# Down projection of a top-2 expert layer: half of its rows on split weights, a second loading queue, and block ends without GpSimd's drain

## The chip, the cores and the metric

One NeuronCore of a Trainium2 chip runs the whole decoder layer as one program. The metric is the device time of an execution in microseconds (us), lower is better. The five engines are PE (TensorE), DVE (VectorE), ACT (ScalarE), POOL (GpSimd) and SP (SyncE, which here only issues DMAs).

## What is computed

A decoder layer on 1024 tokens of 1024 features: a mixer (stick-breaking attention beside gated linear attention), then a mixture of experts, then a last RMSNorm. Only the expert layer matters for the change:

```python
# every token has 2 of 32 experts; the tokens of an expert are padded to whole blocks
def expert_block(args):
    e, x_blk = args
    hidden = jax.nn.silu(x_blk @ exp_w_gate[e]) * (x_blk @ exp_w_up[e])
    return hidden @ exp_w_down[e]          # (block, 512) @ (512, 1024)

yb = lax.map(expert_block, (block_expert, xb))
y = yb.reshape(n_slots, D) * slot_gate[:, None]
out = zeros.at[slot_tok].add(y)
```

Everything is float32. `exp_w_gate` and `exp_w_up` are 1024x512 for an expert, `exp_w_down` 512x1024, 2 MB each.

## The kernel before

The program is a row of blocks (`nc.Block()`), each with one instruction list per engine; at a block's end all engines meet, and POOL first runs an instruction DRAIN. The last three blocks are in `mix_and_route` (output projection, routing), `experts` and `combine` (sum of the two experts' rows, last norm).

`experts` goes over blocks of at most 96 tokens (CAP), 32 of them for these inputs, one an expert. The loop body holds two blocks and runs 15 times; the last two blocks stand behind it. For block b:

- POOL gathers the 96 rows of tokens (`x_g`), PE transposes them (`turn_x`), ACT copies them from PSUM rounded to the single-pass type fp32r (`x_hi`), and DVE subtracts to get the rest (`x_lo`).
- The gate and up weights are split in the same way, in halves of 128x2048: ACT writes `g_hi`/`u_hi`, DVE writes `g_lo`/`u_lo` = raw - hi. PE then makes each product as three fp32r matmuls (hi\*hi, lo\*hi, hi\*lo): 24 matmuls of 128x512 for the gate, 24 for up (`rows`, L1566).
- ACT takes the sigmoid of the gate product, DVE multiplies twice (`gate_mul`, then `up_mul`, which writes `hid`, L1515), PE transposes `hid` (`turn_h`, L1558), ACT copies it to `hidT` (L1451).
- The down projection (`down`, L1590) is plain float32: 4 row groups (KF) x 2 halves of the columns, 8 matmuls, which the compiler makes 16 instructions. ACT moves the result out with the gate factor (`evict`, L1461) and POOL scatters the rows to `y2_dram`.

The order on each engine is written by hand. PE has, for a block: 15 gate matmuls of the next block, `turn_h`, 9 gate matmuls, `down`, 12 up matmuls, `turn_x`, 12 up matmuls:

```python
gate_rows(b + 1, 1 - j, 0, 15)
turn_h(b)
gate_rows(b + 1, 1 - j, 15, 24)
down(b, j, 16 * i + 16)
up_rows(b + 1, 1 - j, 0)
turn_x(j, 16 * i + 32)
up_rows(b + 1, 1 - j, 1)
```

SP loads each half of `w_g` and `w_u` when DVE has made its lower part (semaphores `glo`, `ulo`), and the 2 MB of `w_d` (two buffers) when the down projection before is done (`d_used`).

Of the kernel before, what the change touches and what calls it, by code (L numbers as in the profile page):

```python
# [14 lines left out]
F32 = mybir.dt.float32  # L15
# [922 lines left out]
def mix_and_route(k, c, out_c, cat, tiles, retire):  # L938
# [77 lines left out]

    with nc.Block() as block:
        @block.sync
# [293 lines left out]
def experts(k, c, tables, tiles):  # L1312
# [6 lines left out]
    (w_g, wg, g_in), (w_u, wu, u_in) = weights["g"], weights["u"]  # L1319
    w_d, wd, d_in = sb("w_d", [P, 2, KF, D], F32, c), k["a"]["exp_w_down"][0], [sem(f"e_d_in{m}") for m in range(2)]  # L1320
# [26 lines left out]
    with nc.Block() as block:  # L1347
        @block.sync
        def _(sp):
            def down(j, e):  # L1350
                sp.dma_start(w_d[:, j], wd[bass.ds(e, 1)].rearrange("o (p k) n -> p (o k) n", p=P)).then_inc(d_in[j], 16)
# [6 lines left out]
            down(0, 0)  # L1358
            for m in range(2):
                sp.wait_ge(ulo, m + 1)  # L1360
                load(sp, w_u, wu, 1, m, u_in)
            n_less = sp.value_load(halves[0:1, 1:2], min_val=EXPERTS // 2 - 1, max_val=MAX_HALVES - 1)
            with sp.Fori(0, n_less) as i:
                for j in range(2):
                    b = 2 * i + j
                    e2 = sp.value_load(block_e[0:1, bass.ds(b + 2, 1)], min_val=0, max_val=EXPERTS - 1)
                    e1 = sp.value_load(block_e[0:1, bass.ds(b + 1, 1)], min_val=0, max_val=EXPERTS - 1)
                    for m in range(2):
                        sp.wait_ge(glo, 2 * b + m + 3)
# [62 lines left out]
        def _(act):  # L1432
# [24 lines left out]
            def evict(b, j, i):  # L1457
                act.wait_ge(d_used, b + 2)
# [24 lines left out]
            b = 2 * n_less  # L1483
            u_split(b + 1, 1)
            hid_copy(b)
            sigmoid(b + 1)
            evict(b, 0, n_less)
            hid_copy(b + 1)
            evict(b + 1, 1, n_less)

        @block.vector
        def _(dve):
# [31 lines left out]
            g_split(1, 1)  # L1524
            x_split(1, 1)
            u_split(1, 0)
            n_less = dve.value_load(halves[0:1, 1:2], min_val=EXPERTS // 2 - 1, max_val=MAX_HALVES - 1)
            with dve.Fori(0, n_less) as i:
                for j in range(2):
                    b = 2 * i + j  # L1530
                    up_mul(b)
                    u_split(b + 1, 1)
                    g_split(b + 2, 0)
                    gate_mul(b + 1)
                    g_split(b + 2, 1)
                    x_split(b + 2, j)
                    u_split(b + 2, 0)
            b = 2 * n_less
            up_mul(b)
            u_split(b + 1, 1)  # L1540
            gate_mul(b + 1)
            up_mul(b + 1)

        @block.tensor
        def _(pe):
# [37 lines left out]
            def down(b, j, loaded):  # L1583
                pe.wait_ge(hidT_done, b + 1)
# [9 lines left out]
            pe.sem_inc(d_used, 1)  # L1594
            turn_x(0, 16)
# [32 lines left out]
def combine(k, c, cat):  # L1628
# [77 lines left out]
```

## Time and profile before

| | us |
|---|---|
| median of 3 executions | 1517.08 (1517.06 to 1518.2) |
| the profiled execution | 1505.85 |
| its span, first to last instruction | 1504.1 |
| PE busy in the span | 1271.8 (85%) |
| DVE / ACT / POOL busy | 778.8 / 624.4 / 205.6 |
| mean granted TensorE clock | 0.937 of full speed |

The profiled execution has 1.75 us around its span. The median of the executions without a profile lies 11.2 us above it. `experts` runs from 812 to 1462 us of the span, `combine` behind it. Times within the span are counted from its start. A row of a timeline gives start and length of an instruction; since instructions overlap in an engine's pipeline, the distance of two starts in a dense row ("the pitch") tells the engine's rate better than the length.

### The profile page before, as it was taken

What the parts mean: (1) busy time and instruction counts of PE and PEld (TensorE: products, weight loads), DVE (VectorE), ACT (ScalarE), POOL (GpSimd) and SP (SyncE); (2) the same over time, 40 slices, a digit from 0 to 9 for tenths busy, and PEclk for the clock granted to TensorE, in tenths of its full rate; (3) what the DMA queues carried; (4) which work ended last, traced back from release to release, by engine and by line L of the source; (5) the groups of instructions that cost most, each with busy time, mean ns of one, the idle gap of its engine ahead of it and who ended that gap; (6) DMA issues with size and microseconds to landing.
All of it is one profiled execution on the core that took longest, in us unless ns stands there. A gap on an engine that the chain in (4) does not pass through costs nothing. (4 is left out here: it accounts for less than half of the span.)

```text
span 1504.1 us, 16744 instructions
## 1 busy us (share of the span) xinstructions
PE 1271.8 (85%) x5980; PEld 921.7 (61%) x5980; DVE 778.8 (52%) x786; ACT 624.4 (42%) x695; POOL 205.6 (14%) x222
## 2 busy tenths in 40 slices
PE   4999998868977995769963999999999999999940
PEld 3867676646766685548852666666666666666620
DVE  5163646462357318454466655555555555555407
ACT  6254545444221422231121555555555455555403
POOL 0000000002023004100024022121222221122100
PEclk9999999998998998979975999999999999999975
DMA  5110000002100100072104999999999999999618
GB/s 168 43 29 19 25 1 1 1 3 69 42 14 1 42 14 0 0 294 103 56 29 150 400 368 351 356 342 353 346 340 355 347 338 345 347 357 345 238 42 323
DMA packets 71612, 263.06 MB, mean 175 GB/s; under 512 B 13826, under 2 KB 39444, under 8 KB 51092
## 3 DMA queue, kind: packets, MB, share of 16 engines
q1 hardware_dynamic: 61780, 245.59, 44.4%
q0 software_dynamic: 9792, 16.93, 3.6%
q8 instruction: 26, 0.43, 0.1%
q14 instruction: 14, 0.11, 0.0%
HBM read 249.33 MB, written 21.55 MB: 180 GB/s over the span
## 5 line engine op out<-in xcount | busy, mean ns | idle before, releaser
L1590 PE MATMUL ps<-w_d,hidT 128*96 128x512 f32 x512 | 225.0, 592 | 0.8 <-ACT hidT L1451 0.8
L1496 DVE TENSOR_TENSOR g_lo<-w_g,g_hi 128x2048 fp32r<-128x2048 f32 x62 | 141.7, 2286 | 42.9 <-ACT g_hi L1437 42.9
L1501 DVE TENSOR_TENSOR u_lo<-w_u,u_hi 128x2048 fp32r<-128x2048 f32 x64 | 146.2, 2285 | 27.8 <-ACT u_hi L1443 27.8
L1590 PEld LDWEIGHTS ps<-w_d,hidT 128*96 128x96 f32 x512 | 83.3, 163 | 123.6 <-issue 120.1
L406 DVE TENSOR_TENSOR_SCAN prod<-stay 128x256 f32<-128x256 f32 (+7 forms) x64 | 83.4, 1345 | 86.2 <-ACT beta L358 86.2
L1505 DVE TENSOR_TENSOR x_lo<-ps,x_hi 128x768 fp32r<-128x768 f32 x32 | 30.6, 957 | 187.8 <-ACT x_hi L1447 187.8
L1443 ACT ACTIVATE u_hi<-w_u 128x2048 fp32r<-128x2048 f32 x62 | 118.7, 1914 | 10.6 <-PE ps L1566 7.3
L1437 ACT ACTIVATE g_hi<-w_g 128x2048 fp32r<-128x2048 f32 x62 | 118.1, 1904 | 6.0 <-PE ps L1566 5.9
L1566 PE MATMUL ps<-u_hi,x_hi 128*128 128x512 f32 x256 | 116.3, 454 | 0.0
L1566 PE MATMUL ps<-g_hi,x_hi 128*128 128x512 f32 x256 | 104.8, 409 | 2.0 <-DVE x_lo L1505 2.0
L1566 PE MATMUL ps<-g_lo,x_hi 128*128 128x512 f32 x256 | 101.9, 398 | 0.0
L1566 PE MATMUL ps<-g_hi,x_lo 128*128 128x512 f32 x256 | 101.7, 397 | 0.0
L1566 PE MATMUL ps<-u_lo,x_hi 128*128 128x512 f32 x256 | 101.4, 396 | 0.0
L1566 PE MATMUL ps<-u_hi,x_lo 128*128 128x512 f32 x256 | 101.2, 395 | 0.0
L1461 ACT ACTIVATE y<-ps,where 96x1024 f32<-96x1024 f32 x32 | 35.6, 1112 | 147.6 <-PE ps L1590 147.6
L250 PE MATMUL ps<-h_hi,gw_hi 128*128 128x512 f32 x208 | 83.4, 401 | 12.2 <-DVE gw_lo L710 7.7
L933 POOL DMA_INDIRECT x_g<-h_dram,who x32 | 56.4, 1762 | 216.8 <-DMA where<-slots 198.2
L444 PE MATMUL ps<-h_hi,w_hi 128*128 128x512 f32 x192 | 79.0, 412 | 4.6 <-DVE w_lo L396 4.6
L250 PE MATMUL ps<-h_lo,gw_hi 128*128 128x512 f32 x208 | 82.4, 396 | 0.0
L250 PE MATMUL ps<-h_hi,gw_lo 128*128 128x512 f32 x208 | 82.4, 396 | 0.0
L444 PE MATMUL ps<-h_hi,w_lo 128*128 128x512 f32 x192 | 75.9, 395 | 0.0
L444 PE MATMUL ps<-h_lo,w_hi 128*128 128x512 f32 x192 | 75.6, 394 | 0.0
(272 smaller groups left out, 2285.9 us busy)
## 6 DMA issues: line engine op xcount, KB each, us to landing
w_g<-exp_w_gate SPq DMA_DIRECT2D x64, 1024.0 KB, 6.9
w_u<-exp_w_up SPq DMA_DIRECT2D x64, 1024.0 KB
w_d<-exp_w_down SPq DMA_DIRECT2D x32, 2048.0 KB, 11.4
gw_raw<-w_in SPq DMA_DIRECT2D x13, 512.0 KB
w_raw<-w_in SPq DMA_DIRECT2D x12, 512.0 KB, 3.9
xt<-x SPq DMA_DIRECT2D x8, 512.0 KB, 6.6
x_g<-x SPq DMA_DIRECT2D x8, 512.0 KB, 3.4
h_dram<-h SPq DMA_DIRECT2D x8, 512.0 KB, 2.6
```

The lines of the kernel that those rows point to most:

```text
L250: mm = pe.matmul(out, w[:, kd, :], h[:, kd, cols], start=(n == 0), stop=(n == 3 * KD - 1))
L406: dve.tensor_tensor_scan(prod[:, h, T - nk:T][:, ::-1], x, x, 1.0, ALU.mult, ALU.bypass)\
L444: mm = pe.matmul(out, w[:, t % 2, x // 3, :], h[:, x // 3, cols], start=(x == 0), stop=(x == 3 * KD - 1))
L933: pool.indirect_dma_start(x_g[0:CAP, j, :], None, k["h2_dram"][:, :], bass.IndirectOffsetOnAxis(ap=who[j][0:CAP, 0:1], axis=0), bounds_che ...
L1437: act.activation(g_hi[:, 4 * m:4 * m + 4], w_g[:, 4 * m:4 * m + 4], ACT.Copy).then_inc(ghi, 1)
L1443: act.activation(u_hi[:, 4 * m:4 * m + 4], w_u[:, 4 * m:4 * m + 4], ACT.Copy).then_inc(uhi, 1)
L1461: act.activation(y[j][0:CAP, :], ps[0:CAP, 2:4, :].rearrange("p b n -> p (b n)"), ACT.Copy, scale=where[j][:].bitcast(F32)[0:CAP, 2:3]).th ...
L1496: dve.tensor_tensor(g_lo[:, part], w_g[:, part], g_hi[:, part].bitcast(F32), ALU.subtract).then_inc(glo, 1)
L1501: dve.tensor_tensor(u_lo[:, part], w_u[:, part], u_hi[:, part].bitcast(F32), ALU.subtract).then_inc(ulo, 1)
L1505: dve.tensor_tensor(columns(x_lo[j]), turned_x(), columns(x_hi[j]).bitcast(F32), ALU.subtract).then_inc(xlo_done, 1)
L1566: mm = pe.matmul(out, x_[:, n // 3, :], w_[:, n // 3, :], start=(n == 0), stop=(n == 3 * KD - 1))
L1590: mm = pe.matmul(ps[0:CAP, 2 + m, :], hidT[:, f, :], w_d[:, j, f, cols], start=(f == 0), stop=(f == KF - 1))
```

## The change

1. Row groups 0 and 1 of the down projection are made on split operands. `w_s` (one buffer, 128x2048) takes their weights; ACT makes `s_hi` from it and DVE `s_lo`; the transposed hidden rows of these groups are split as well, into `hT_hi` (ACT) and `hT_lo` (DVE), with 96 columns each. Each of these products is three fp32r matmuls. Row groups 2 and 3 stay plain, with `w_d` now half as large (two buffers of 128x2048) and `hidT` too.
2. ACT asks for the plain half of the weights, in its own queue behind `evict`, and loads the expert's number for it from `block_e`; SP asks for `w_s`, between the two halves of `w_g`.
3. The last three blocks of the program are opened with `no_gpsimd_drain=True`.

```diff
-    with nc.Block() as block:
+    with nc.Block(no_gpsimd_drain=True) as block:      (mix_and_route, experts, combine)
...
                     for m in range(2):
                         sp.wait_ge(glo, 2 * b + m + 3)
                         load(sp, w_g, wg, e2, m, g_in)
-                    sp.wait_ge(d_used, b + 1)
-                    down(1 - j, e1)
+                        if m == 0:
+                            sp.wait_ge(slo, b + 1)
+                            sp.dma_start(w_s[:], wd[bass.ds(e1, 1)].rearrange("o (p k) n -> p (o k) n", p=P)[:, 0:HF])\
+                              .then_inc(s_in, 16)
...
             def hid_copy(b):
                 act.wait_ge(hturned, b + 1)
-                act.activation(hidT[:], turned_h(), ACT.Copy).then_inc(hidT_done, 1)
+                act.activation(hT_hi[:], turned_h()[:, 0:HF], ACT.Copy).then_inc(hidT_done, 1)
+                act.activation(hidT[:], turned_h()[:, HF:KF], ACT.Copy).then_inc(hidT_done, 1)
+
+            def s_split(b, first=False):
+                act.wait_ge(s_in, 16 * b + 16)
+                if not first:
+                    act.wait_ge(d_used, b)
+                act.activation(s_hi[:], w_s[:], ACT.Copy).then_inc(shi, 1)
...
                     evict(b, j, i)
+                    e2 = act.value_load(block_e[0:1, bass.ds(b + 2, 1)], min_val=0, max_val=EXPERTS - 1)
+                    act.dma_start(w_d[:, j], wd[bass.ds(e2, 1)].rearrange("o (p k) n -> p (o k) n", p=P)
+                                  [:, HF:KF]).then_inc(d_in[j], 16)
                     x_split(b + 2, j)
+                    s_split(b + 1)
                     u_split(b + 2, 0)
...
+            def h_split(b):
+                dve.wait_ge(hidT_done, 2 * b + 2)
+                dve.tensor_tensor(hT_lo[:], turned_h()[:, 0:HF], hT_hi[:].bitcast(F32), ALU.subtract).then_inc(hTlo_done, 1)
+
+            def s_split(b):
+                dve.wait_ge(shi, b + 1)
+                dve.tensor_tensor(s_lo[:], w_s[:], s_hi[:].bitcast(F32), ALU.subtract).then_inc(slo, 1)
...
                     up_mul(b)
                     u_split(b + 1, 1)
+                    h_split(b)
                     g_split(b + 2, 0)
                     gate_mul(b + 1)
                     g_split(b + 2, 1)
                     x_split(b + 2, j)
+                    s_split(b + 1)
                     u_split(b + 2, 0)
...
-                for m in range(D // HALF):
-                    cols = slice(m * HALF, (m + 1) * HALF)
-                    for f in range(KF):
-                        mm = pe.matmul(ps[0:CAP, 2 + m, :], hidT[:, f, :], w_d[:, j, f, cols], start=(f == 0),
-                                       stop=(f == KF - 1))
+                for f in range(HF):
+                    for m in range(D // HALF):
+                        cols = slice(m * HALF, (m + 1) * HALF)
+                        pe.matmul(ps[0:CAP, 2 + m, :], hidT[:, f, :], w_d[:, j, f, cols], start=(f == 0), stop=False)
+                pe.wait_ge(hTlo_done, b + 1)
+                pe.wait_ge(slo, b + 1)
+                for f in range(HF):
+                    for n, (x_, w_) in enumerate(((hT_hi, s_hi), (hT_hi, s_lo), (hT_lo, s_hi))):
+                        for m in range(D // HALF):
+                            cols = slice(m * HALF, (m + 1) * HALF)
+                            mm = pe.matmul(ps[0:CAP, 2 + m, :], x_[:, f, :], w_[:, f, cols], start=False,
+                                           stop=(f == HF - 1 and n == 2))
```

Three places of the order that results, the loop body in each case.

DVE before, from the first product with the sigmoid (`gate_mul`) to the product that writes `hid` for `turn_h` (`up_mul`, the last row but one):

```order
L1510 TENSOR_TENSOR hid<-ps,hid 96x512
L1494 REGISTER_ALU
L1496 TENSOR_TENSOR g_lo<-w_g,g_hi 128x2048
L1504 REGISTER_ALU
L1505 TENSOR_TENSOR x_lo<-ps,x_hi 128x8x96
L1501 TENSOR_TENSOR u_lo<-w_u,u_hi 128x2048
L1515 TENSOR_TENSOR hid<-ps,hid 96x512
L1501 TENSOR_TENSOR u_lo<-w_u,u_hi 128x2048
```

The same place of DVE with the change:

```order
L1532 TENSOR_TENSOR hid<-ps,hid 96x512
L1516 REGISTER_ALU
L1518 TENSOR_TENSOR g_lo<-w_g,g_hi 128x2048
L1526 REGISTER_ALU
L1527 TENSOR_TENSOR x_lo<-ps,x_hi 128x8x96
L1545 TENSOR_TENSOR s_lo<-w_s,s_hi 128x2048
L1523 TENSOR_TENSOR u_lo<-w_u,u_hi 128x2048
L1537 TENSOR_TENSOR hid<-ps,hid 96x512
L1523 TENSOR_TENSOR u_lo<-w_u,u_hi 128x2048
L1541 TENSOR_TENSOR hT_lo<-ps,hT_hi 128x192
```

`s_lo` has come between `x_lo` and the `u_lo` that stands ahead of `up_mul`, and `hT_lo` behind it.

ACT before, from the sigmoid to the copy of the turned hidden rows:

```order
L1455 ACTIVATE hid<-ps 96x512
L1437 ACTIVATE g_hi<-w_g 128x2048
L1459 ISA
L1461 ACTIVATE y<-ps,where 96x1024
L1446 REGISTER_ALU
L1447 ACTIVATE x_hi<-ps 128x8x96
L1443 ACTIVATE u_hi<-w_u 128x2048 x2
L1451 ACTIVATE hidT<-ps 128x384
```

ACT with the change:

```order
L1477 ACTIVATE y<-ps,where 96x1024
L1498 ISA
L1498 TENSOR_LOAD block_e
L1498 ISA x2
L1499 ISA
L1499 DMA w_d<-exp_w_down 128x2048
L1455 REGISTER_ALU
L1456 ACTIVATE x_hi<-ps 128x8x96
L1467 ACTIVATE s_hi<-w_s 128x2048
L1452 ACTIVATE u_hi<-w_u 128x2048 x2
L1460 ACTIVATE hT_hi<-ps 128x192
L1461 ACTIVATE hidT<-ps 128x192
```

Between `evict` and `x_hi` there is now a load of a register and an issue of a DMA, and between `x_hi` and `u_hi` the pass that writes `s_hi`.

SP before, the loads of one block:

```order
L1344 ISA
L1344 DMA w_g<-exp_w_gate 128x2048
L1369 REGISTER_ALU
L1344 ISA
L1344 DMA w_g<-exp_w_gate 128x2048
L1351 ISA
L1351 DMA w_d<-exp_w_down 128x4096
L1344 DMA w_u<-exp_w_up 128x2048 x2
```

SP with the change:

```order
L1349 ISA
L1349 DMA w_g<-exp_w_gate 128x2048
L1380 ISA
L1380 DMA w_s<-exp_w_down 128x2048
L1376 REGISTER_ALU
L1349 ISA
L1349 DMA w_g<-exp_w_gate 128x2048
L1349 DMA w_u<-exp_w_up 128x2048 x2
```

The second half of `w_g` now stands behind the load of `w_s`, whose wait is for `s_lo`.

## Rows read from the trace of the kernel before

**Rows 1.** By stretch: its us; PE, PEld, DVE, ACT, POOL busy; clock, DMA share, GB/s.

```profile
610.00:620.00 10.00, 8.38 (x50) 6.60 (x48) 3.89 (x10) 0.00 (x0) 0.00 (x0) 1.00 0.00 0
836.00:845.00 9.00, 9.00 (x26) 4.32 (x26) 6.79 (x4) 5.32 (x4) 0.00 (x0) 1.00 1.01 429
880.00:1400.00 520.00, 512.29 (x2019) 337.73 (x2018) 292.24 (x185) 270.39 (x212) 102.63 (x107) 1.00 0.95 349
```

**Rows 2.** Timeline, one block on PE: start, length, engine, line, operation.

```profile
909.35 0.40 PE L1566 MATMUL ps<-g_hi,x_hi 128*128 128x512 f32 x1
...
912.85 0.60 PE L1558 MATMUL ps<-ident,hid 96*128 96x96 f32 x4
...
915.42 7.03 PE L1590 MATMUL ps<-w_d,hidT 128*96 128x512 f32 x16
921.89 0.80 PE L1566 MATMUL ps<-u_hi,x_hi 128*128 128x512 f32 x1
...
932.09 0.61 PE L1558 MATMUL ps<-ident,hid 96*128 96x96 f32 x4
```

**Rows 3.** Timeline of ACT and DVE in the same block, around `up_mul`.

```profile
916.16 1.90 ACT L1437 ACTIVATE g_hi<-w_g 128x2048 fp32r<-128x2048 f32 x1
...
925.96 0.81 ACT L1447 ACTIVATE x_hi<-ps 128x768 fp32r<-128x768 f32 x1 [2.22 <-PE ps L1551]
926.67 1.91 ACT L1443 ACTIVATE u_hi<-w_u 128x2048 fp32r<-128x2048 f32 x1
...
928.61 2.29 DVE L1501 TENSOR_TENSOR u_lo<-w_u,u_hi 128x2048 fp32r<-128x2048 f32 x1 [0.84 <-ACT u_hi L1443]
930.82 0.68 DVE L1515 TENSOR_TENSOR hid<-ps,hid 96x512 f32<-96x512 f32 x1
932.74 0.49 ACT L1451 ACTIVATE hidT<-ps 128x384 f32<-128x384 f32 x1 [1.96 <-PE ps L1558]
```

**Rows 4.** Timeline of the last block, where PE waits for `hid`.

```profile
1431.23 1.11 ACT L1461 ACTIVATE y<-ps,where 96x1024 f32<-96x1024 f32 x1 [6.41 <-PE ps L1590]
...
1436.71 0.69 DVE L1515 TENSOR_TENSOR hid<-ps,hid 96x512 f32<-96x512 f32 x1 [11.17 <-PE ps L1566]
1437.45 0.72 PE L1558 MATMUL ps<-ident,hid 96*128 96x96 f32 x4 [0.78 <-DVE hid L1515]
```

**Rows 5.** Weight loads of plain and single-pass matmuls (min/median/max ns).

```profile
L1292 PEld LDWEIGHTS ps<-wr,h2T x112: 188/192/333, 705.4 to 780.2; 128*128 128x128 f32 x112
L1566 PEld LDWEIGHTS ps<-g_hi,x_hi x256: 187/188/330, 816.4 to 1423.1; 128*128 128x128 f32 x128
L1590 PEld LDWEIGHTS ps<-w_d,hidT 128*96 128x96 f32 x512 | 83.3, 163 | 123.6 <-issue 120.1
```

**Rows 6.** Timeline of the first block's `up_mul` and `turn_h`.

```profile
827.39 0.81 ACT L1447 ACTIVATE x_hi<-ps 128x768 fp32r<-128x768 f32 x1 [0.57 <-PE ps L1551]
...
833.84 0.72 PE L1558 MATMUL ps<-ident,hid 96*128 96x96 f32 x4
```

**Rows 7.** The ends of `mix_and_route` (L1017) and `experts` (L1347): ns, start us.

```profile
L1017 POOLq DRAIN  x1: 6578/6578/6578, 805.7 to 805.7; - x1
...
L1347 POOLq DRAIN  x1: 10352/10352/10352, 1452.0 to 1452.0; - x1
...
806.72 0.96 POOL L933 DMA_INDIRECT x_g<-h_dram,who  x1 [0.30 <-issue]
812.63 0.81 SPq L1344 DMA_DIRECT2D w_g<-exp_w_gate  x2
...
DMA to landing us min/median/max: 4.3/4.7/10.7
```

**Rows 8.** `w_d`'s loads (L1351): to landing, issue on SP (ns); SP's register loads.

```profile
DMA to landing us min/median/max: 8.4/11.4/15.2
...
L1366 SPq TENSOR_LOAD <-block_e x30: 263/267/278, 822.1 to 1384.7; - x30
...
L1351 SPq DMA_DIRECT2D w_d<-exp_w_down x32: 332/333/432, 813.5 to 1412.0; - x32
```

More of the change, by code:

```diff
@@ L1015, in pieces @@
         return ap.rearrange("p (a n) -> p a n", n=P)
-    with nc.Block() as block:
+    with nc.Block(no_gpsimd_drain=True) as block:
         @block.sync
@@ L1319, in experts @@
     (w_g, wg, g_in), (w_u, wu, u_in) = weights["g"], weights["u"]
-    w_d, wd, d_in = sb("w_d", [P, 2, KF, D], F32, c), k["a"]["exp_w_down"][0], [sem(f"e_d_in{m}") for m in range(2)]
+    wd, d_in, s_in = k["a"]["exp_w_down"][0], [sem(f"e_d_in{m}") for m in range(2)], sem("e_s_in")
+    HF = KF // 2
+    w_s = sb("w_s", [P, HF, D], F32, c)
+    s_hi, s_lo = (sb(n, [P, HF, D], F32R, c) for n in ("s_hi", "s_lo"))
+    w_d = sb("w_d", [P, 2, HF, D], F32, c)
+    hT_hi, hT_lo = (sb(n, [P, HF, CAP], F32R, c) for n in ("hT_hi", "hT_lo"))
     (g_hi, g_lo, ghi, glo), (u_hi, u_lo, uhi, ulo) = parts["g"], parts["u"]
@@ L1324, in experts @@
     hid = sb("hid", [P, FF], F32, c)
-    hidT = sb("hidT", [P, KF, CAP], F32, c)
+    hidT = sb("hidT", [P, HF, CAP], F32, c)
     y = [sb(f"y{j}", [P, D], F32, c) for j in range(2)]
     scattered, where_in = ([sem(f"e_{n}{j}") for j in range(2)] for n in ("scattered", "where"))
-    names = "e_made e_turn e_xhi e_xlo e_g e_u e_sig e_gated e_hid e_hturn e_hT e_d e_y e_passed".split()
+    names = "e_made e_turn e_xhi e_xlo e_g e_u e_sig e_gated e_hid e_hturn e_hT e_d e_y e_passed e_shi e_slo e_hTlo".split()
     (made, turned, xhi_done, xlo_done, g_used, u_used, sig_done, gated, hid_done, hturned, hidT_done, d_used, y_done,
-     passed) = (sem(n) for n in names)
+     passed, shi, slo, hTlo_done) = (sem(n) for n in names)
     MADE = 4
@@ L1345, in load, with down @@
                      [:, m * n:(m + 1) * n]).then_inc(landed[m], 16)
-    with nc.Block() as block:
+    with nc.Block(no_gpsimd_drain=True) as block:
         @block.sync
         def _(sp):
-            def down(j, e):
-                sp.dma_start(w_d[:, j], wd[bass.ds(e, 1)].rearrange("o (p k) n -> p (o k) n", p=P)).then_inc(d_in[j], 16)
+            def down(j):
+                sp.dma_start(w_d[:, j], wd[j].rearrange("(p k) n -> p k n", p=P)[:, HF:KF]).then_inc(d_in[j], 16)
             for j in range(2):
@@ L1357, in _ @@
                 load(sp, w_g, wg, 1, m, g_in)
-            down(0, 0)
+            sp.dma_start(w_s[:], wd[0].rearrange("(p k) n -> p k n", p=P)[:, 0:HF]).then_inc(s_in, 16)
+            down(0)
             for m in range(2):
@@ L1361, in _ @@
                 load(sp, w_u, wu, 1, m, u_in)
+            down(1)
             n_less = sp.value_load(halves[0:1, 1:2], min_val=EXPERTS // 2 - 1, max_val=MAX_HALVES - 1)
@@ L1365, in _ @@
                     b = 2 * i + j
+                    e1 = sp.value_load(block_e[0:1, bass.ds(b + 1, 1)], min_val=0, max_val=EXPERTS - 1)
                     e2 = sp.value_load(block_e[0:1, bass.ds(b + 2, 1)], min_val=0, max_val=EXPERTS - 1)
-                    e1 = sp.value_load(block_e[0:1, bass.ds(b + 1, 1)], min_val=0, max_val=EXPERTS - 1)
                     for m in range(2):
@@ L1376, in _ @@
             e1 = sp.value_load(block_e[0:1, bass.ds(2 * n_less + 1, 1)], min_val=0, max_val=EXPERTS - 1)
-            sp.wait_ge(d_used, 2 * n_less + 1)
-            down(1, e1)
+            sp.wait_ge(slo, 2 * n_less + 1)
+            sp.dma_start(w_s[:], wd[bass.ds(e1, 1)].rearrange("o (p k) n -> p (o k) n", p=P)[:, 0:HF]).then_inc(s_in, 16)
         @block.gpsimd
@@ L1457, in evict @@
             def evict(b, j, i):
-                act.wait_ge(d_used, b + 2)
+                act.wait_ge(d_used, b + 1)
                 act.wait_ge(where_in[j], 16 * i + 16)
@@ L1469, in _ @@
             x_split(1, 1)
+            s_split(0, True)
             u_split(1, 0)
@@ L1525, in _ @@
             x_split(1, 1)
+            s_split(0)
             u_split(1, 0)
@@ L1536, in _ @@
                     x_split(b + 2, j)
+                    s_split(b + 1)
                     u_split(b + 2, 0)
@@ L1540, in _ @@
             u_split(b + 1, 1)
+            h_split(b)
             gate_mul(b + 1)
+            s_split(b + 1)
             up_mul(b + 1)
+            h_split(b + 1)
         @block.tensor
@@ L1583, in down @@
             def down(b, j, loaded):
-                pe.wait_ge(hidT_done, b + 1)
+                pe.wait_ge(hidT_done, 2 * b + 2)
                 pe.wait_ge(y_done, b + 2)
                 pe.wait_ge(d_in[j], loaded)
-                for m in range(D // HALF):
-                    cols = slice(m * HALF, (m + 1) * HALF)
-                    for f in range(KF):
-                        mm = pe.matmul(ps[0:CAP, 2 + m, :], hidT[:, f, :], w_d[:, j, f, cols], start=(f == 0),
-                                       stop=(f == KF - 1))
+                for f in range(HF):
[10 more added lines that the diff above has]
+                                           stop=(f == HF - 1 and n == 2))
                 mm.then_inc(d_used, 1)
-            pe.sem_inc(d_used, 1)
             turn_x(0, 16)
@@ L1644, in pieces @@
         return ap.rearrange("p (a n) -> p a n", n=P)
-    with nc.Block() as block:
+    with nc.Block(no_gpsimd_drain=True) as block:
         @block.sync
```

## The prediction

> **What bounds the kernel now.** The table of stretches comes first: from 880 to 1400 us PE is busy 512.29 of 520 us at the full granted clock, ACT 270 and DVE 292 [rows 1]. So the expert loop goes at PE's pace. DMA is busy 0.95 of that time at 349 GB/s, which looks like a second bound, but 836 to 845 us moved 429 GB/s [rows 1]: there is room.
>
> The timeline of PE gives the period: `turn_h` starts at 912.85 and again at 932.09, so a block takes 19.24 us. Within it the down projection goes from 915.42 to where the next up matmul really begins, 921.89 + 0.80 - 0.40 = 922.29 (its row is twice as long as its neighbours because it waits in the pipe for the last plain one): 6.87 us for 16 instructions, 0.429 each. The single-pass matmuls have a pitch of 0.233: 15 of them, from 909.35 to 912.85, fill the 3.50 us ahead of `turn_h` [rows 2].
>
> The timeline of ACT and DVE shows how near the next thing is. `up_mul` ends at 930.82 + 0.68 = 931.50, and PE, busy until then, takes its result at 932.09 [rows 2, 3]. **The cover is 0.59 us.** Ahead of `up_mul` lies a chain without play: `x_hi` 925.96, `u_hi` 926.67, its end 928.58, `u_lo` 928.61, `up_mul` 930.82, 2.21 behind `u_lo` [rows 3].
>
> **Down projection on PE.** Four plain matmuls remain (8 instructions) and twelve split ones come. 8 x 0.429 + 12 x 0.233 = 3.43 + 2.80 = 6.24 us against 6.87: **-0.63 us a block**, 32 blocks, -20.2 us. No single-pass matmul of the trace has a stationary side of 96 columns; all have 128. Bounds of the pitch: half of the plain instruction, 0.215, below (-0.22 us a block), and the plain instruction's own 0.429 above (+2.35). I take 0.233, the row with the same type and the same moving side.
>
> Here a rule speaks against the change. The weight loads of 128 single-pass columns took 188 ns and of 128 plain ones 192, those of 96 plain ones 163 [rows 5]: type and width buy hardly anything. The Trainium skill ("TensorE: Matmul & The Clock Gate", section "Weight-path perf modes — Fast Weight Load (FWL) and DoubleRow") says that the fast weight load wants exactly 128 columns and a type other than FP32. By that the 96-column operands would lose a fast load that the other single-pass matmuls have; the rows show no such fast load to lose. What it would cost if loads came into the open is a rival below.
>
> **The new passes ahead of `up_mul`.** ACT now writes `s_hi` between `x_hi` and `u_hi`, and DVE `s_lo` between `x_lo` and `u_lo`; both have the shape of the u passes. With block times as before: `s_hi` takes the place of `u_hi` (926.67 to 928.58), `s_lo` that of `u_lo` (928.61), `u_hi` runs beside it and ends about 930.5, `u_lo` starts one pass later, at 928.61 + 2.21 = 930.82, and `up_mul` at 933.03, done at 933.71 [rows 3]. PE takes a result 0.05 us after its end (1436.71 + 0.69 = 1437.40 to 1437.45) [rows 4], so `turn_h` starts at 933.76 instead of 932.09: **+1.67 us a block**. PE is in order and everything behind `turn_h` moves with it, the next `turn_x` and `x_hi` too, so the wait comes again in each block and is not caught up. Thirty blocks (1 to 30): +50.1 us. In block 0 `x_hi` started at 827.39; by the same distances (933.76 - 925.96 = 7.80) `turn_h` starts at 835.19 instead of 833.84 [rows 6]: +1.35. In the last block there is room: `up_mul` waits for the up matmuls anyway and starts 5.48 us behind the `evict` of the block before [rows 4], and `evict`, `s_hi` and `s_lo` (1.1 + 1.9 + 2.3) take 5.3 of that. The new period is 19.24 - 0.63 + 1.67 = 20.28 us.
>
> **Costed at nothing, and their cover.** `hidT` becomes two copies, between 0.49 (together as before) and 0.98 us (two whole ones); `hidT` was asked for 0.65 us behind `turn_h`'s start and is needed 2.57 behind it (912.85 to 915.42) [rows 2, 3]: covered by the nine gate matmuls; in the last block there are none, +0.2. `hT_lo`, at most the 0.68 of `up_mul`, stands behind a `u_lo` on DVE and is needed only after 3.4 us of plain matmuls. ACT's register load and DMA issue are 0.27 and 0.33 us where SP does them [rows 8], with the register steps under 1 us; ACT sat idle 2.22 us there, ahead of `x_hi` [rows 3]. If that cover went, each us would go straight into the chain above. POOL's gathers and scatters keep their order and gain 1 us a block.
>
> **The loads.** SP asks for `w_s` and, behind it, the second half of `w_g` only when `s_lo` is done, 930.9. ACT's pass over that half stood at 916.16 [rows 3], so it is wanted at 916.16 + 19.24 + 1.67 = 937.1; but ACT has nothing else then until `evict`, at 915.42 + 19.24 + 1.67 + 6.24 = 942.6. Two megabytes landed in 11.4 us (8.4 to 15.2) [rows 8]: at 942.3; pass until 944.2, `evict` and issue until 946.2, and `x_hi` is due at 925.96 + 20.28 = 946.24. It just fits at the median, which was taken behind 2 MB of other loads; here the queue is nearly empty. So: nothing, with a rival. The other loads have 10 us and more.
>
> **The drains.** At the end of `experts` POOL reaches its DRAIN at 1452.0, last of all engines and with its waits for the scatters over, and stays in it 10.35 us [rows 7]: -10.35. At the end of `mix_and_route` it is 6.58 us from 805.7, but the last gather is issued at 806.72 and lands about 4.3 later, near 811.0, which SP waits for; SP issued at 812.63 [rows 7]. Between -1.6 (SP) and -2.9 (PE needs only the gather before, 0.96 + 0.30 us earlier); I take -2. `combine`: nothing shown at its end, 0.
>
> **The sum:** -20.2 + 50.1 + 1.35 + 0.2 - 10.35 - 2 = +19.1 us on the profiled execution, 1505.85 to 1525. Its span lies 1.75 below that, and the median of the executions 11.2 above; nothing in the profile says that this distance changes, so the median goes from 1517.1 to **1536**. A measurement of this kernel can tell about 0.2%, 3 us.
>
> **Rivals.**
>
> - *The split hides (faster).* If the two new passes found a gap, so that `up_mul` came under 0.59 us later, only the gains would stay: 1517.1 - 20.2 - 12.35 = 1484.5. The place is `turn_h`; the point is a stall of 1.1 us a block ((20.2 + 12.35) / 30), below which the kernel is faster. For it: DVE is idle 44% of the loop [rows 1]. Against it: the one idle stretch in the chain, 0.84 us ahead of `u_lo`, is spent waiting for ACT, which gets a pass more as well [rows 3]. 8%, with 4% more for ending within 0.2%.
> - *Late loads or a slow issue on ACT.* If the half of `w_g` lands 1 us later than reckoned, or ACT's issue costs 3 us and not 1, each block loses 1 us more: 1536 + 30 = 1566; at the longest landing seen, 15.2, it would be 3.8 us a block. For it: the chain above has no play at the median. 12%. The Trainium skill ("DMA: Bandwidth & Descriptors", section "Issuing engines are not separate DMA queues") says that transfers asked for by SP and by ACT share the same 16 DMA engines; by it ACT's queue brings no bandwidth, and the sum counts none.
> - *Narrow operands are slow.* With 96 columns the split matmuls go at the plain pitch: 12 x 0.196 x 32 = +75, 1611; or each shows its load of 163 ns: 12 x 0.163 x 32 = +63, 1599. For it: no row has this shape. Against: width did not matter in loads. 4%.
> - *The drain's work only moves.* Then 10 to 12 us stay: 1548. 4%.
> - The clock: 1.67 us of PE waiting in 20.28 is a busy share of 92%; between 610 and 620 us PE was busy 8.38 of 10 and kept the granted clock at 1.00, the 2.4 GHz level [rows 1]. No case of its own.
>
> **How the numbers follow.** The forecast has 68%. Its own bounds: pitch 0.215 (-7), stall 1.5 to 1.8 (-5 to +4), the first drain (-1, 0): 1522 to 1545. Reaching for 8 in 10, the range takes in the case of the drain and the first two thirds of a us of lateness: 1521 to 1557. Faster by over 0.2%: 0.08; within 0.2%: 0.04; slower: 0.88.
>
> **What would show it.** In the new profile: `turn_h` with a wait for DVE's `hid` of about 1.7 us in each block, nothing of the kind elsewhere on PE; period 20.3; the twelve split matmuls at 0.23 us; `s_lo` directly behind `s_hi`; `combine`'s first load 0.7 us after POOL's last wait. I am wrong if PE shows no wait at `turn_h` (then the order did not do what I read), if ACT's idle time ahead of `x_hi` is gone, or if the split matmuls have another pitch.

## The result, and the profile after

| | before | after |
|---|---|---|
| median of 20 executions each, us | 1517.64 (1506.79 to 1523.89) | 1523.76 (1518.26 to 1528.27) |
| the profiled execution, us | 1505.85 | 1519.82 |
| its span, us | 1504.1 | 1518.1 |
| PE / DVE / ACT busy, us | 1271.8 / 778.8 / 624.4 | 1262.5 / 860.7 / 684.1 |
| mean granted TensorE clock | 0.937 | 0.937 |

The ratio is 1.0041 (95% interval 1.0025 to 1.0057): the change costs 6 us, 0.4%. The forecast had the right sign, but was 12 us too high. The two profiled executions lie 14.0 us apart, so there are two gaps to explain: from 19.1 (the sum) to 14.0, and from 14.0 to 6.1.

The table of stretches of the kernel after, columns as in [rows 1]:

```profile
880.00:1400.00 520.00, 482.49 (x2046) 339.89 (x2045) 347.91 (x229) 306.85 (x256) 99.38 (x103) 1.00 0.89 335
```

Against [rows 1] PE is busy 30 us less in the same 520 us, while ACT and DVE are busy 36 and 56 us more. PE no longer bounds the loop at every moment. The clock stays at 1.00, the 2.4 GHz level, although PE now stops once in every block.

Where it stops is shown by its list of waits in the expert loop (engine, line that waited and what for: us in total, times, longest), kernel after:

```profile
PE ps L1594 <- DVE hid L1537: 48.0, 31, 3.0
```

The 3.0 is block 0's; the other thirty are about 1.5 each.

The timeline of one block after, all engines, answers to [rows 2] and [rows 3]:

```profile
910.06 0.81 ACT L1456 ACTIVATE x_hi<-ps 128x768 fp32r<-128x768 f32 x1 [2.36 <-PE ps L1587]
910.77 1.91 ACT L1467 ACTIVATE s_hi<-w_s 128x2048 fp32r<-128x2048 f32 x1
...
912.71 2.29 DVE L1545 TENSOR_TENSOR s_lo<-w_s,s_hi 128x2048 fp32r<-128x2048 f32 x1 [0.84 <-ACT s_hi L1467]
...
914.92 2.28 DVE L1523 TENSOR_TENSOR u_lo<-w_u,u_hi 128x2048 fp32r<-128x2048 f32 x1
...
915.96 0.40 PE L1602 MATMUL ps<-g_lo,x_hi 128*128 128x512 f32 x1
...
917.12 0.68 DVE L1537 TENSOR_TENSOR hid<-ps,hid 96x512 f32<-96x512 f32 x1
...
917.85 0.72 PE L1594 MATMUL ps<-ident,hid 96*128 96x96 f32 x4 [1.50 <-DVE hid L1537]
...
920.55 3.60 PE L1626 MATMUL ps<-w_d,hidT 128*96 128x512 f32 x8
...
923.58 1.02 PE L1633 MATMUL ps<-s_hi,hT_hi 128*96 128x512 f32 x2
923.83 1.92 ACT L1446 ACTIVATE g_hi<-w_g 128x2048 fp32r<-128x2048 f32 x1 [2.39 <-DMA w_g<-exp_w_gate]
924.43 0.63 PE L1633 MATMUL ps<-s_lo,hT_hi 128*96 128x512 f32 x2
924.90 0.62 PE L1633 MATMUL ps<-s_hi,hT_lo 128*96 128x512 f32 x2
...
926.75 0.40 PE L1602 MATMUL ps<-u_hi,x_hi 128*128 128x512 f32 x1
...
927.10 1.11 ACT L1477 ACTIVATE y<-ps,where 96x1024 f32<-96x1024 f32 x1 [1.35 <-PE ps L1633]
...
938.22 0.72 PE L1594 MATMUL ps<-ident,hid 96*128 96x96 f32 x4 [1.50 <-DVE hid L1537]
```

Follow it from above. `s_lo` starts 1.94 us behind `s_hi`, `u_lo` directly behind `s_lo`, `up_mul` (L1537) 2.20 later; it ends at 917.80 and `turn_h` starts at 917.85. The last gate matmul ahead of it began at 915.96, so with the pitch of 0.233 `turn_h` was due at 916.19: it is 1.66 us late. The down projection goes from 920.55 to 926.75, 6.20 us. Two starts of `turn_h` are 20.37 us apart. Of the other things that could have stopped PE, the second half of `w_g` lands late, and ACT waits 2.39 us for it at 923.83; but ACT is done at 925.75 and then waits 1.35 us for PE before `evict`. This wait is real and costs nothing.

The ends of the two blocks on POOL, kernel after (instructions by line, min/median/max ns, start), against [rows 7]:

```profile
L1017 POOLq EVENT_SEMAPHORE  x2: 17/17/17, 806.8 to 806.9; - x2
...
L1352 POOLq COMPARE_BRANCH  x1: 41/41/41, 1476.7 to 1476.7; - x1
L1352 POOLq EVENT_SEMAPHORE  x2: 17/17/17, 1476.8 to 1476.9; - x2
```

and the start of `combine` on SP in its timeline:

```profile
1477.05 0.33 SPq L1693 DMA_DIRECT2D c_ya<-y_dram  x1
```

No DRAIN is left on POOL, and `combine`'s first load follows the branch that ends POOL's list by about 0.35 us.

To see where the 14.0 us between the profiled executions lie, take the 32 starts of `evict` (min/median/max ns, first and last start). First the kernel before:

```profile
L1461 ACT ACTIVATE y<-ps,where x32: 1110/1112/1113, 843.7 to 1446.1; 96x1024 f32<-96x1024 f32 x32
```

and after:

```profile
L1477 ACT ACTIVATE y<-ps,where x32: 1110/1114/1117, 845.6 to 1470.8; 96x1024 f32<-96x1024 f32 x32
```

| stretch, us | before | after | difference | the sum had |
|---|---|---|---|---|
| to the end of the linear attention (L573) | 645.0 | 645.6 | +0.6 | 0 |
| to the first `evict` | 198.7 | 200.0 | +1.3 | -1.3 |
| 30 distances of `evict` | 587.5 | 611.0 | +23.5 | +31.2 |
| the last distance | 14.8 | 14.2 | -0.6 | -0.4 |
| last `evict` to the end of the span | 58.0 | 47.3 | -10.8 | -10.4 |
| all | | | +14.0 | +19.1 |

One line is out by much: the loop. After, its distances are 20.23 and 20.51 in strict alternation, mean 20.37, where 20.28 was forecast. Before, they aren't the 19.24 that one pair of rows gave, but 587.5 / 30 = 19.58: most are 19.11 or 19.38, with longer ones, up to 21.2, every second or third block. That is 10 us above 30 distances of 19.25, and PE's waits in the loop before hold 7.7 of them:

```profile
PE ps L1551 <- DMA x_g<-h_dram,who: 7.7, 9, 1.7
```

`turn_x` waits for gathered tokens that land too late. After, it never does in the loop.

The other line that is out is the way to the first `evict`, +1.3 where the sum had -1.3. The rows of block 0, kernel after, ACT and PE, and the table of the stretch behind them:

```profile
830.01 1.92 ACT L1452 ACTIVATE u_hi<-w_u 128x2048 fp32r<-128x2048 f32 x1 [2.11 <-DMA w_u<-exp_w_up]
...
834.91 0.88 PE L1594 MATMUL ps<-ident,hid 96*128 96x96 f32 x4 [3.01 <-DVE hid L1537]
...
835.20:838.50 3.30, 3.30 (x11) 2.73 (x11) 2.12 (x2) 1.57 (x3) 0.00 (x0) 0.50 1.01 427
```

PE begins block 0 2.9 us earlier than before, counted from L573 (its first gate matmul starts at 814.11 - 645.6 = 168.5 after, at 816.36 - 645.0 = 171.4 before), but the pass over `w_u` waits for the load, so the first `turn_h` waits 3.01 us, and right behind that wait the granted clock is 0.50, the 1.2 GHz level. Before, PE has no wait there and the clock is 1.00 ([rows 1], 836 to 845 us).

### The profile page after: what moved, and what is told of

Its sections match the earlier page's. It is cut to its first block and busy times, and to the rows that moved or that the text cites. A ratio compares the mean times of both kernels' runs of the same rounds, so it can differ in the third digit from the quotient of the medians.

```text
span 1518.1 us, 17429 instructions
## 1 busy us (share of the span) xinstructions
PE 1262.5 (83%) x6108; PEld 944.8 (62%) x6108; DVE 860.7 (57%) x850; ACT 684.1 (45%) x760; POOL 209.9 (14%) x222
## 5 line engine op out<-in xcount | busy, mean ns | idle before, releaser
L1452 ACT ACTIVATE u_hi<-w_u 128x2048 fp32r<-128x2048 f32 x62 | 115.0, 1903 | 2.8 <-DMA w_u<-exp_w_up 2.8
L1626 PE MATMUL ps<-w_d,hidT 128*96 128x512 f32 x256 | 115.1, 592 | 0.8 <-ACT hidT L1461 0.8
L1602 PE MATMUL ps<-u_hi,x_hi 128*128 128x512 f32 x256 | 103.7, 405 | 0.0
L1545 DVE TENSOR_TENSOR s_lo<-w_s,s_hi 128x2048 fp32r<-128x2048 f32 x32 | 73.3, 2292 | 33.3 <-ACT s_hi L1467 33.2
L1398 POOL DMA_INDIRECT y_dram<-y,where x32 | 31.4, 982 | 369.1 <-ACT y L1477 352.6
L933 POOL DMA_INDIRECT x_g<-h_dram,who x32 | 60.1, 1878 | 131.7 <-DMA where<-slots 124.2
L1626 PEld LDWEIGHTS ps<-w_d,hidT 128*96 128x96 f32 x256 | 41.6, 163 | 55.6 <-issue 52.1
```

The costliest lines, as they stand in the source:

```text
L933: pool.indirect_dma_start(x_g[0:CAP, j, :], None, k["h2_dram"][:, :], bass.IndirectOffsetOnAxis(ap=who[j][0:CAP, 0:1], axis=0), bounds_che ...
L1398: pool.indirect_dma_start(k["y2_dram"][:, :], bass.IndirectOffsetOnAxis(ap=where[j][0:CAP, 1:2], axis=0), y[j][0:CAP, :], None, bounds_che ...
L1452: act.activation(u_hi[:, 4 * m:4 * m + 4], w_u[:, 4 * m:4 * m + 4], ACT.Copy).then_inc(uhi, 1)
L1545: dve.tensor_tensor(s_lo[:], w_s[:], s_hi[:].bitcast(F32), ALU.subtract).then_inc(slo, 1)
L1602: mm = pe.matmul(out, x_[:, n // 3, :], w_[:, n // 3, :], start=(n == 0), stop=(n == 3 * KD - 1))
```

## Experiments

Two theories stood at the start. One: the loop before is longer than the block that the prediction measured, since `turn_x` waits for the gather; the new wait at `turn_h` gives the gather its time back, and these waits vanish. The other: the profiled execution of before is simply a short one.

In all runs "before" is the kernel before, run beside the experiment on the same chip; medians in us, ratios with their 95% interval.

### The kernel before once more

> The kernel before, unchanged, profiled once more. Its first profiled execution took 1505.85 us and its median is 1517.6. Theory A (the first profile was a fast draw: executions differ inside the span, in the loads of the expert layer): this one's span is several us off 1504.1, most likely 8 to 15 longer, and the surplus lies between the first load of an expert and the end of experts, as waits for DMA, with the stages before it equal within 1 us. Theory B (the draw differs in the front, by the clock of TensorE): the surplus lies before 770 us of the span, at a lower granted clock.

Measured: median 1515.72, span 1514.1, 10.0 longer than the first profile's. Waits of PE in its loop:

```profile
PE ps L1551 <- DMA x_g<-h_dram,who: 11.0, 10, 1.9
```

Its 31 distances of `evict` take 607.0 us, where the first profile had 602.3 (1446.06 - 843.73). Its first part, up to L573, took 650.2, where the first profile had 645.0. So both theories hold a part: the first profile was short by 5 us in code that the change doesn't touch, and by 5 in the loop, in waits for the gather. The first part goes with the granted clock, as theory B had it (before, then this run, up to about L573):

```profile
0.00:645.00 645.00, 527.03 (x2960) 411.62 (x2960) 309.65 (x353) 249.58 (x365) 61.05 (x62) 0.95 0.10 27
0.00:650.00 650.00, 536.30 (x2960) 418.19 (x2960) 309.41 (x353) 249.86 (x365) 61.19 (x62) 0.93 0.09 27
```

The same 2960 matmuls keep PE busy 9.3 us longer at 0.93 instead of 0.95. Over the ten other profiles of this study, with the same code up to L573, its end lies between 645.3 and 650.2, 648.0 on average; what lets the clock differ there from run to run is not shown.

### Each part alone

> Part 3 of the change alone (no_gpsimd_drain in the last three blocks), down projection as before. If the drains are worth what the two traces say at the ends of mix_and_route and experts (6.6 and 10.4 us, of which the first gather takes back up to 4): -12 to -16 us, ratio 0.990 to 0.992. If the drain's work only moves to a later place: 0 to -3 us.

```diff
-    with nc.Block() as block:
+    with nc.Block(no_gpsimd_drain=True) as block:      (mix_and_route, experts, combine)
```

Measured: 1505.68, ratio 0.9937 (0.9916 to 0.9959), 9.5 us faster by the ratio. From the last `evict` to the end it takes 47.45 us, not 58.04. At the end of `mix_and_route` the engines meet at 805.5 us, in the first profile at 812.5, with the end of L573 nearly the same (645.3 and 645.0). But the first `evict` does not come earlier: 199.3 us behind L573, against 198.7. PE starts its first gate matmul about 4 us earlier and then waits 2.56 us at the first `turn_h`, since ACT's pass over `w_u` ahead of it waits 3.45 us for the load. Its loop takes 608.1. The ratio misses the expected 0.990 to 0.992 by what the drain of `mix_and_route` was to bring.

> The change without part 3: the drains are back, the split and ACT's loads stay. By the order read ahead (period 19.24 to 20.3 us): +25 to +31 us, ratio 1.017 to 1.020. If the split costs only what the medians of before and after leave for it without a gain by the drains: +6 us, ratio 1.004.

The edit is the change without `no_gpsimd_drain=True`. Measured: 1535.1, ratio 1.0129 (1.0103 to 1.0155), 20 us slower: less than the 25 to 31 of the one theory, and far more than the 6 of the other. Its 31 distances take 626.9 us, against 607.0 in the second profile of before: +19.9, and that is nearly all of the difference. PE's waits in its loop:

```profile
PE ps L1594 <- DVE hid L1537: 45.1, 30, 1.6
```

The two changes of the ratio add up to 1.0066 (-0.0063 and +0.0129), some 0.0034 either way, which holds the 1.0041 of the whole change. The drains carry the gain, that of `experts` all that can be told from noise, and the split the loss.

### The split moved to where DVE and ACT have time

If the price is the two passes ahead of `up_mul`, they can go behind it.

> The change with s_split moved on ACT and DVE from ahead of u_split(b+2, 0) to behind u_split(b+1, 1), ahead of the hidden rows' split, and SP's load of w_s behind the two loads of w_u; ACT's wait for d_used in s_split falls away, since evict of the block before has made it. Stall theory (up_mul is late by one pass of 128x2048 on DVE, less a cover of 0.6 us): turn_h waits no more, period 18.6 us, 1.7 us a block less than with the change, -50 us against it and -26 to -33 us against before, ratio 0.979 to 0.983. Rival (the loop is slower because loads come late, w_g's second half above all): the period falls by under 0.5 us and PE then waits for something else.

```diff
                     u_split(b + 1, 1)
+                    s_split(b)
                     hid_copy(b)           (ACT; on DVE likewise between u_split(b + 1, 1) and h_split(b))
...
                     x_split(b + 2, j)
-                    s_split(b + 1)
                     u_split(b + 2, 0)     (ACT and DVE)
...
                 act.wait_ge(s_in, 16 * b + 16)
-                if not first:
-                    act.wait_ge(d_used, b)
...
                     for m in range(2):
                         sp.wait_ge(ulo, 2 * b + m + 3)
                         load(sp, w_u, wu, e2, m, u_in)
+                    sp.wait_ge(slo, b + 1)
+                    sp.dma_start(w_s[:], ...)       (was between the halves of w_g)
```

A bad miss: 1618.08, ratio 1.0694 (1.0660 to 1.0728). The wait at `turn_h` is gone from all blocks but the first, as expected, and half of the distances are 18.46. The other half are 27.7 to 29.6, but for a last one of 23.8. PE's waits:

```profile
PE ps L1584 <- DMA x_g<-h_dram,who: 101.5, 13, 8.9
PE ps L1591 <- DVE hid L1534: 3.0, 1, 3.0
```

The timeline of such a block, DVE and POOL, with the `turn_x` behind it:

```profile
996.28 2.28 DVE L1520 TENSOR_TENSOR u_lo<-w_u,u_hi 128x2048 fp32r<-128x2048 f32 x1
...
998.10 8.83 POOL L933 DMA_INDIRECT x_g<-h_dram,who  x1 [5.62 <-DMA where<-slots]
998.48 2.28 DVE L1542 TENSOR_TENSOR s_lo<-w_s,s_hi 128x2048 fp32r<-128x2048 f32 x1
1000.68 0.35 DVE L1538 TENSOR_TENSOR hT_lo<-ps,hT_hi 128x192 fp32r<-128x192 f32 x1
1000.95 2.28 DVE L1515 TENSOR_TENSOR g_lo<-w_g,g_hi 128x2048 fp32r<-128x2048 f32 x1
1003.15 0.68 DVE L1529 TENSOR_TENSOR hid<-ps,hid 96x512 f32<-96x512 f32 x1
1003.75 2.28 DVE L1515 TENSOR_TENSOR g_lo<-w_g,g_hi 128x2048 fp32r<-128x2048 f32 x1
...
1015.90 1.38 PE L1584 MATMUL ps<-ident,x_g 96*128 96x96 f32 x7 [7.20 <-DMA x_g<-h_dram,who]
```

The gather's issue on POOL, which takes 1.0 us elsewhere, starts beside `u_lo` and ends at 1006.93, 0.9 us behind the end of DVE's dense row of subtractions (1003.75 + 2.28 = 1006.03). Its tokens land about 9 us later, and PE stands for 7.2. With this in mind the kernel before reads differently. Its timeline, DVE, POOL and the `turn_x` behind:

```profile
935.06 2.29 DVE L1496 TENSOR_TENSOR g_lo<-w_g,g_hi 128x2048 fp32r<-128x2048 f32 x1 [1.36 <-ACT g_hi L1437]
935.19 3.06 POOL L933 DMA_INDIRECT x_g<-h_dram,who  x1 [7.46 <-DMA where<-slots]
937.27 0.68 DVE L1510 TENSOR_TENSOR hid<-ps,hid 96x512 f32<-96x512 f32 x1
...
944.50 0.70 PEld L1551 LDWEIGHTS ps<-ident,x_g 96*128 96x128 f32 x8 [0.43 <-DMA x_g<-h_dram,who]
```

Here too a gather starts beside a `g_lo`, takes three times as long and ends at 938.25, behind it. POOL started it as late as 935.19 because it had waited 7.46 us for its small lookups of `who` and `where`.

### Early lookups: is the gather's start the cause?

The table of tokens for block b + 3 is looked up right behind the issue of gather b + 2, once gather b + 1, which used the same buffer, has landed. So each gather can start right behind `turn_x`, while DVE is idle. In the cut the steps of the semaphore `passed` and the first lookup ahead of the loop are left out.

> The kernel before with POOL's order changed and nothing else: the list of a block's tokens (who) is asked for one block earlier, so the gather of x_g is issued right behind the scatter, while DVE is idle. Theory (the gather waits for DVE's passes that read two operands in SBUF, lands late every other block, and turn_x waits for it: mean distance of evicts 19.58 to 19.77 us where a block of work is 19.24): every distance 19.1 or 19.38, all gathers near 1.0 us on POOL, no wait of PE for x_g, -10 to -16 us, ratio 0.989 to 0.993. Rival (the surplus comes from something else, late weights for one): gathers early but the long distances stay, ratio above 0.997.

```diff
...
+                    pool.wait_ge(who_in[j], 16 * i + 32)
+                    pool.wait_ge(turned, b + 1)
+                    gather(j)
+                    pool.wait_ge(gathered[1 - j], 16 * i + 16 + 16 * j)
+                    look(who[1 - j], who_in[1 - j], row_of(b + 3))
-                    pool.wait_ge(gathered[j], 16 * i + 16)
-                    look(who[j], who_in[j], row_of(b + 2))
                     pool.wait_ge(scattered[j], 16 * i + 16)
                     look(where[j], where_in[j], row_of(b))
-                    pool.wait_ge(who_in[j], 16 * i + 32)
-                    pool.wait_ge(turned, b + 1)
-                    gather(j)
...
```

Measured, with this edit on the kernel before: 1501.82, ratio 0.9919 (0.9890 to 0.9947). A gather of its timeline, with the `turn_x` it follows:

```profile
946.96 0.82 PE L1554 MATMUL ps<-ident,x_g 96*128 96x96 f32 x8
947.63 1.01 POOL L933 DMA_INDIRECT x_g<-h_dram,who  x1 [0.31 <-issue]
```

No wait for `x_g` is left, PE is busy all of 880 to 1400 us, and the distances are 19.11 and 19.38 in strict alternation. Their 31 take 592.2 us; that is the loop that the prediction had taken for the kernel before. The edit makes the gather start some 9 us earlier and takes away its slow issue at once, so it doesn't tell how much of the loss each of them made.

> The changed kernel with the same early gather. Theory (with the change the stall at turn_h of 1.5 us a block has taken the place of the waits for x_g, so there is nothing left to win): distances stay 20.23 and 20.51, ratio to before 1.002 to 1.006, as without it. Rival (late gathers still cost the changed kernel): it gets faster by 5 us or more, ratio under 1.001.

Measured, with the same edit on the kernel after: 1524.77, ratio 1.0075 (1.0049 to 1.0100). The ratio lies a little above the expected 1.002 to 1.006, which its interval reaches into. The distances stay 20.23 and 20.51, and the 31 take 625.2, as without the edit. The gathers (min/median/max ns):

```profile
L933 POOL DMA_INDIRECT x_g<-h_dram,who x32: 970/1006/1036, 809.6 to 1422.0; - x32
```

In the kernel after they took 970/1784/3617. Shorter gathers are worth nothing there, because `turn_h`'s wait of 1.66 us covers them.

### Both together

> The late split (s_split behind u_split(b+1, 1) on ACT and DVE) with the early gather. Theory of the gather (the late split closed DVE's gaps at the time of the gather, which then took 8 to 9 us on POOL in every second block and held up turn_x): both parities now at 18.45 us, no wait at turn_h, experts about 39 us shorter than in before, and 10 by the drains: ratio 0.967 to 0.973. Rival (the long blocks of 29 us come from the loads): they stay, ratio above 1.05.

The edits of the late split and of the early lookups, on the kernel after. Measured: **1470.24, ratio 0.9712 (0.9683 to 0.9741)**, 43 us faster than the kernel before, where each of the two edits alone leaves the kernel after slower than before (1618.08 and 1524.77). First its table of stretches:

```profile
880.00:1400.00 520.00, 520.00 (x2240) 374.76 (x2239) 377.78 (x251) 335.90 (x279) 84.56 (x111) 1.00 0.96 360
```

then its gathers:

```profile
L933 POOL DMA_INDIRECT x_g<-h_dram,who x32: 969/1006/2187, 809.0 to 1371.8; - x32
```

PE does not stand at all; the distances are 18.46 and 18.73, mean 18.6, where 19.24 - 0.63 = 18.61 is what the down projection's term gives. So that term is right; in the kernel after it is in the period as well, with the new wait on top (19.24 - 0.63 + 1.67). Two passes of 1.9 and 2.3 us in another place are worth 54.5 us here (against the run with the early lookups alone, 1524.77).

### The drains once more, and the cause of the slow gather

> The kernel before with the early gather and without the three drains. With the waits for x_g gone, what the drains are worth stands alone: at the end of experts 10.4 us, at the end of mix_and_route 6 to 7 less the 3 to 4 that PE then waits for the first gather. So -13 to -14 us against the early gather alone and -24 to -26 against before: ratio 0.983 to 0.985. If the drains are worth only what the run with them alone left over (9.5 us), 0.986 to 0.988.

The early lookups and the three block ends, without the split: 1493.51, ratio 0.9850 (0.9814 to 0.9886). Against the early lookups alone (0.9850 / 0.9919 = 0.9930) that is 10.5 us, with 7 either way. The profiles are sharper: from the last `evict` to the end it is 47.1 us against 57.7, which is the drain of `experts`, and the first `evict` stands 200.5 us behind L573, against 198.5 with the drain of `mix_and_route`. Here too PE begins earlier, by 2.7 us, and then waits 2.9 at the first `turn_h`. A third pair, the kernel after against the split alone, has 200.0 against 201.5. So leaving that drain out moved the first `evict` by +2.0, +0.6 and -1.5 us, where the prediction had -1.6 to -2.9: no gain that these profiles can tell.

> The late split with the old, late gather (the run with 29 us in every second block), but DVE's s_lo takes its second operand from PSUM (bank 6, read four times) instead of s_hi from SBUF; s_lo then holds other values, so the down projection of two row groups is left wrong; number, size and order of all instructions are the same. Theory (a gather on POOL waits only for those passes of DVE that read both operands in SBUF): the gathers that took 8 to 9 us get done beside s_lo, under 4 us each, the long blocks fall from 29 us to under 21, time under 1530. Rival (POOL is held up by any busy DVE, or the long blocks have another cause): gathers stay at 8 to 9 us and the time near 1618.

```diff
-                dve.tensor_tensor(s_lo[:], w_s[:], s_hi[:].bitcast(F32), ALU.subtract)
+                dve.tensor_tensor(s_lo[:] ..., w_s[:] ..., bank(k, 6).unsqueeze(1).to_broadcast([P, 4, HALF]), ALU.subtract)
```

The late split without the early lookups, with one edit: DVE's pass takes its second operand from PSUM and not from `s_hi`, with the same shape and length; this changes the values of `s_lo`, and so of row groups 0 and 1 of the down projection. Measured, in two executions: 1471.64, ratio 0.9702 (0.9657 to 0.9747), where the same order with `s_hi` had 1618.08. Its timeline at the place:

```profile
988.60 2.28 DVE L1542 TENSOR_TENSOR s_lo<-w_s,ps 128x2048 fp32r<-128x2048 f32 x1
989.90 1.01 POOL L933 DMA_INDIRECT x_g<-h_dram,who  x1 [7.02 <-DMA where<-slots]
990.80 0.35 DVE L1538 TENSOR_TENSOR hT_lo<-ps,hT_hi 128x192 fp32r<-128x192 f32 x1
991.07 2.28 DVE L1515 TENSOR_TENSOR g_lo<-w_g,g_hi 128x2048 fp32r<-128x2048 f32 x1
```

The gather's issue starts in the middle of a DVE pass of the same length and takes 1.01 us. So it isn't DVE being busy that holds POOL, but DVE reading both of its operands from SBUF. The hold has a sharp end: of the 352 gathers in the eleven profiles 123 took over 1.1 us on POOL, and every one of them ends 0.89 or 0.90 us behind the end of such a pass (938.25 and 1006.93 above are two); the other 229 took 1.04 at most.

The Trainium skill ("SBUF — State Buffer", section "Who interferes with whom") says that a DVE instruction with two SBUF inputs contends with a GpSimd instruction that reads SBUF; the 8.83 and the 1.01 us agree. The same section infers that such a subtraction leaves GpSimd's making of DMA descriptors alone. POOL's plain lookups agree. One in the kernel after with early lookups lies wholly inside such a pass and takes no longer than elsewhere:

```profile
874.74 2.29 DVE L1548 TENSOR_TENSOR s_lo<-w_s,s_hi 128x2048 fp32r<-128x2048 f32 x1 [0.84 <-ACT s_hi L1470]
875.14 0.53 POOL L929 DMA_DIRECT2D where<-slots  x1 [1.51 <-issue]
```

The eleven profiles have 35 such lookups, none above 0.54 us. The indirect gather was held. Its list of rows lies in SBUF, and that reading this list is what waits is an inference; no run gathers without one.

## Why the prediction was right or wrong

**Right, by its own steps.** *The new passes ahead of `up_mul`*: 1.66 us late, 1.67 forecast, at the place named, in each block. *Down projection on PE*: 6.20 us, 6.24 forecast (its 3.43 + 2.80 make 6.23). Behind 8 x 0.429 of plain ones the twelve split matmuls have from 923.98 to 926.75, 0.231 each, and the rival of narrow operands is gone. Their weight loads, in the kernel after (min/median/max ns), where 128 columns take 188 [rows 5]:

```profile
L1633 PEld LDWEIGHTS ps<-s_hi,hT_hi x128: 161/162/163, 842.1 to 1469.3; 128*96 128x96 f32 x128
```

*The new period*: 20.37 for 20.28; from `turn_h` to `down` it takes 2.70 us and not 2.57, since a `turn_h` that starts behind a wait takes 0.72 and not 0.60, as [rows 4] and [rows 2] had it already. *The loads*: the late half of `w_g` was absorbed, with 1.35 us to spare; the rival of late loads is gone. ACT's issue fitted its idle time (kernel after, ns); ACT's queue as a part by itself was not tried:

```profile
L1499 ACTq DMA_DIRECT2D w_d<-exp_w_down x30: 344/349/402, 846.4 to 1436.9; - x30
```

*The drain of `experts`*: -10.35 forecast, -10.8 between the profiles, -9.5 and -10.5 in the runs; its work did not move elsewhere. *The clock* stayed at 1.00 in the loop.

**Wrong: "a block takes 19.24 us".** This was read off one pair of rows (912.85 to 932.09), a pair without a wait. The loop's mean was 19.58 in the same profile, and 19.74 and 19.77 in the second profile of before and in the run of the block ends: 10, 15 and 16 us in all above 30 undisturbed distances of 19.25. A block after takes 20.37, so the loss of a block is 0.6 to 0.8 us and not 1.04. The mean was to be had from the first and last `evict`; [rows 2] could not show it. The step that hid it was one of those costed at nothing: "POOL's gathers and scatters keep their order and gain 1 us a block". They gained it, and it was worth 10 us in the profile, 15 in the second profile of before, and 12 in the medians (the early lookups on the kernel before, 0.9919), since the new wait lies ahead of `turn_x` and the gather lands under it. A saving was overlooked, not a cost.

**Wrong: "nothing in the profile says that this distance changes".** The median of before lies 11.8 us above its profiled execution, that of after 3.9. The waits for the gather vary from execution to execution (5 us more in both later profiles), and they exist only before. With them, 14.0 - 5 - 0.6 (the first part, which the change doesn't touch) gives 8.4, where 6.1 was measured, with 2.4 either way.

**Wrong, small: the drain of `mix_and_route`, -2.** The prediction let all that PE begins earlier reach the end. PE did begin about 3 us earlier, but the load of `w_u` did not land early enough, and the first `turn_h` waited 2.6 to 3.3 us in the runs without that drain. The term of +1.35 for block 0 went under in this wait.

**The range.** That 1523.8 lies inside 1521 to 1557 is luck: the lower end stood for a faster pitch and a shorter stall, and neither came. The prediction's own bounds (-7, -5 to +4, -1 to 0 on 1536) make 1523 to 1540, not 1522 to 1545.

**The rival "the split hides"** failed as stated, but its price was right: once the passes stand elsewhere and the gather is early, the split brings 21 us (0.9850 without it, 0.9712 with it, 7 either way; by the distances 19.25 - 18.59, 0.66 a block), where the term said 20.2.

What stays open: in the late split the issue on POOL was held through `hT_lo` and `gate_mul`, which have an operand in PSUM, but leave only 0.19 and 0.52 us between the passes from SBUF, less than the 0.89 that every held issue still takes. Whether a longer gap would have let it through was not tried. Why the clock in the front of the program differs from run to run was not tried either.

## What to carry to other kernels

A period read off two starts is the period of a block without accidents: divide first and last start of an `evict` by their number before you price a change of a block, and list the waits that make the difference, because a new stall swallows older waits that lie behind it. Where an order is written by hand, ask of each new pass in front of the instruction that PE waits for whether it could stand behind it, and then what it meets there: here the split cost 20 us with its two passes in one place, over 100 in another, and gained about 20 in that second place once the gather no longer met them.

## What the runs showed of the hardware

- An indirect gather issued by POOL (96 rows) takes 1.0 us. When it starts beside a subtraction of DVE with both operands in SBUF it can be held, and then ends 0.89 or 0.90 us behind that pass (123 of 352 gathers): 3.1 us beside one pass, 7.7 to 9.3 in a dense row of them. With one operand of the pass beside it in PSUM it took 1.01. Plain lookups by POOL inside such passes took their usual 0.5 us.
- POOL's DRAIN at the end of a block took 10.35 us behind a loop with some 130 of its DMAs, and leaving it out gave all of that back. That of 6.58 us ahead of a block whose first loads must land let PE begin about 3 us earlier, and PE then waited 2.6 to 3.3 us at the first `turn_h`; where the first `evict` came, it was worth nothing clear.
- A wait of PE of 1.66 us in every 20.37 left the granted clock at 1.00. Single waits could do otherwise: behind the 3.01 us at the first `turn_h`, and behind 1.60 us at the same place with the split alone, it was 0.50 in the next 3.3 us that were looked at. Waits of 7 to 9 us in every second block brought it to 0.90 on the mean, between the two levels, as the late split's table of stretches shows:

```profile
880.00:1400.00 520.00, 434.29 (x1757) 312.73 (x1756) 297.41 (x198) 265.08 (x220) 152.82 (x88) 0.90 0.79 288
```
